# Moving taps of a 31-tap convolution on VectorE from the query and key units into the steps of a top-64 choice

## The chip, the cores and the metric

The kernel runs on one NeuronCore of a Trainium2 chip. A core has a matrix engine (PE, TensorE, with its weight loads as PEld), a vector engine (DVE), a scalar engine (ACT), a general engine (POOL, GpSimd) and a queue engine that issues the DMAs (SP). Each runs its own list of instructions in order and waits for the others by semaphores. The metric is the device time of one execution in microseconds; lower is better.

## What is computed

The reference chains two blocks on a sequence of 256 tokens with 1024 channels. The first block (two layers of modulated attention and feed-forward) is not touched. The second block has two layers; each projects the normed input into many branches. Cut to what matters here:

```python
def second_block(x, positions, ...):
    for l in range(DEPTH):                       # DEPTH = 2
        h = rms_norm(x, g_mix[l])
        proj = h @ w_in[l]
        aq, ak, av, iq, ik, iw, glu_in, cc_in, sb_in, gate_in = jnp.split(proj, offs, axis=-1)
        qa = partial_rope(rms_norm(aq..., g_qa[l]), positions)     # the same for ka
        qi = partial_rope(iq..., positions); ki = partial_rope(rms_norm(ik, g_kidx[l])...)
        y_a = dsa_attention(qa, ka, va, qi, ki, iw) @ w_oa[l]
        glu_a, glu_b = jnp.split(glu_in, 2, axis=-1)
        u = causal_dwconv(glu_a * jax.nn.sigmoid(glu_b), cb_conv_w[l], cb_conv_b[l])   # 31 taps
        y_b = jax.nn.silu(layer_norm(u, cb_ln_g[l], cb_ln_b[l])) @ w_ob[l]
        gb, gc, xc = jnp.split(cc_in, 3, axis=-1)
        y_c = (gb * causal_dwconv(gc * xc, cc_conv_w[l])) @ w_oc[l]                    # 3 taps
        y_d = stick_breaking_attention(...) @ w_od[l]
        ...
```

`dsa_attention` scores all keys by small index heads, keeps the 64 best keys of each query (`lax.top_k`) and does a softmax attention over those. The kernel turns the choice into a mask that is added to the logits.

## The kernel before

Every weight matrix comes from HBM as units of 128 x 2048 float32 values (1 MB, `raw`). ACT rounds a unit to `w_hi` (L1156), DVE subtracts to get the remainder `w_lo` (L1612), and PE multiplies three times for each tile: `h_hi` by `w_hi` (L716), `h_lo` by `w_hi` (L717), `h_hi` by `w_lo` (L718). A unit has 48 such matmuls. There are three slots of `w_hi` and of PSUM banks `ps`, and four of `raw`. ACT and DVE do the split of unit t+2 (`split_ahead`) at the start of their own work on unit t, in program order.

The order of work is a list of stages, the same for each engine, written by `plan_second` for each of the two layers: `glu` (4 units), `cc` (4 and 2), two query units and two key units (`heads`, tiles `aq` and `ak`, which both lie in buffers that the profile calls `spare`), one unit of index queries (`iq`), half a unit of index keys (`ik`), a tiny unit `iw`, two value units (`av`), `select`, four units of plain projections, two of values (`sv`), four of gates, the softmax attention over the chosen keys (`soft`), stick-breaking attention, `layernorm` and so on.

In a `heads` unit ACT copies the product to `kept` (L1324) and squares it, PE makes column sums (L894) and the rotation (L900), ACT makes the reciprocal root `hr`, and DVE multiplies by the cosine (L1875), and one unit later by the sine (L1894, `rope_t`), adds (L1899) and scales by `hr` (L1908). `kept` has two buffers: the copy of unit j waits for L1908 of unit j-2. PE may write a `ps` slot again when L1894 has read it.

The 31-tap convolution works on 512 channels, four tiles of 128. POOL does tiles 2 and 3 in one go from the end of `glu`: for each tap two products (L2354, `cb_product`) and a sum over both (L2360, `cb_sum`). DVE does tiles 0 and 1: for each tap two multiply-add instructions (L2191, L2188 for the first tap) on `cb_sum`, put between its other work by `conv_taps`. How many taps stand at each unit is the tuple of `plan_second`. After its 31 taps POOL goes on with the 3-tap convolution of `cc` (L2354 and L2360 on `cc_sum` and `cc_product`, then L2384, L2386, L2327 with the output `oc_lo`). `cc_product` lies over `cb_in`, the input of the long convolution, so POOL first waits until DVE has done all its taps:

```python
pool.wait_ge(S["conv_first"], s.conv.b["conv_first"] + 2 * CB_TAPS)      # cc on POOL
...
if s.out == "oa":
    dve.wait_ge(S["cc_out"], b["cc_out"])                                # soft on DVE
```

The second wait stands ahead of the first `logits` (L2038) of the softmax attention on DVE.

In `select` DVE sums the scores of two blocks of queries (L2116) and then makes 22 steps on each, called by `each`: eight times MAX8 (L2147), with MATCH_REPLACE8 (L2149) between them, and seven closing steps that make the mask. Odd turns 1 to 15 are the eight MAX8. After each even turn stands the split of one of the ten units that PE multiplies meanwhile (four plain, two value, four gate units, `behind`).

Of the kernel before, what the change touches and what calls it, by code (L numbers as in the profile page):

```python
# [48 lines left out]
CB_TAPS = 31  # L49
# [137 lines left out]
def build(nc, x_t, vecs, consts, positions, cond_rows, ada_first, ada_t, pre_wi, pre_wo, post_wi, post_wo, a_w_qkv, a_w_o, b_w_qkv, b_w_o,  # L187
          w_in, w_oa, w_ob, w_oc, w_od, w_merge, w_gate, w_up, w_down, out):

    def cols_of(w, col0, width, k0=0, kc=KC):  # L190
        def src(j):
            return [(0, w[k0 * P:(k0 + kc) * P, :].rearrange("(k p) m -> p k m", p=P)
                     [:, :, bass.ds(col0 + j * width, width)])]
        return src

    def two_of(wa, ca, wb, cb):
        def src(j):
            return [(0, wa.rearrange("(k p) m -> p k m", p=P)[:, :, bass.ds(ca + j * P, P)]),
                    (P, wb.rearrange("(k p) m -> p k m", p=P)[:, :, bass.ds(cb + j * P, P)])]
        return src  # L200

    unit_done, hi_ready, lo_ready = (nc.alloc_semaphore(n) for n in ("unit_done", "hi_ready", "lo_ready"))
    stages, counts = [], {}
# [30 lines left out]
    def add(run, filler=()):  # L234

        run.t0 = len(units)
        units.extend((run, j) for j in range(run.n))
        run.free = "psum_read_" + run.by
        run.f0 = counts.get(run.free, 0)
        psum_users.extend((run.free, run.f0 + j + 1) for j in range(run.n))  # L240
        counts[run.free] = run.f0 + run.n
        for j in range(run.n):
            program.extend(("chunk", a.first + k) for a, k in share_of(filler, j, run.n))
            program.append(("unit", run.t0 + j))
        return run
# [149 lines left out]
    def plan_second(l, x):  # L395
# [5 lines left out]
        g = Stage("glu", run=add(Run("glu", 4, KC, 2 * P, two_of(w, OFF["glu"], w, OFF["glu"] + 512), "dve", 2)), l=l, h=h)  # L401
        g.takes(glu_sig=4, conv_pad=1, conv_first=2 * CB_TAPS, conv_steps=CB_TAPS, conv_steps_product=CB_TAPS - 1)
        c = Stage("cc", pair=add(Run("cc", 4, KC, 2 * P, two_of(w, OFF["cc"] + 512, w, OFF["cc"] + 1024), "dve", 2)),
                  run=add(Run("cb", 2, KC, 2 * P, cols_of(w, OFF["cc"], 2 * P), "act")), l=l, h=h)
        c.conv = g
        c.takes(cc_gate=4, cc_pad=1, cc_steps=CC_TAPS, cc_steps_product=CC_TAPS - 1, cc_full=4, cc_hi=4, cc_out=4)
        ahead = [len(stages) - 1]
# [10 lines left out]
        Stage("iw", run=add(Run("iw", 1, KC, HEADS2, cols_of(w, OFF["iw"], HEADS2), "act")), h=h)  # L418
        v = value_units(Run("av", 2, KC, 2 * P, cols_of(w, OFF["av"], 2 * P), "act"), 2, "av")
        tap = 0  # L420
        for st, per in zip([c, *stages[ahead[0] + 1:]], (2, 3, 3, 0, 0, 1, 3)):
            runs = (c.pair.n + c.run.n) if st is c else st.run.n
            st.taps = (g, tap, per)
            tap = min(tap + per * runs, CB_TAPS)
        assert tap == CB_TAPS
        sel = Stage("select", waits=[("head_done", k.b["head_done"] + 1), ("psum_read_act", v.run.f0 + 2)])
        sel.takes(iw_turned=1, iw_kept=1, idx_scores=nt * HEADS2, idx_relu=nt * HEADS2, idx_sum=nt * HEADS2, top_steps=nt * 22, sel_mask=nt)

        q = Stage("plain", run=add(Run("sq", 4, KC, 2 * P, cols_of(w, OFF["sb"], 2 * P), "act")), h=h,
# [149 lines left out]
    def con(name):  # L579
        if name in ANGLES:  # L580
            return angles[:, ANGLES.index(name), :]
        o, w = CON[name]
        return con_sb[:, o:o + w]
# [38 lines left out]
    def next_split(u):  # L622

        return Unit(*split_unit(u.t0 + 2)) if u.t0 + 2 < len(units) else None
# [37 lines left out]
    with block:  # L662
# [941 lines left out]
        def _(dve):  # L1604
            def split(u):

                if u is None:
                    return
                n = u.run.kc * u.run.cols
                dve.wait_ge(hi_ready, u.count)  # L1610
                whole, _, _ = raw_of("unit", u.t0)
                nc.vector.tensor_tensor(w_lo[u.low][:, 0:n], whole[:, 0:n], w_hi[u.slot][:, 0:n].bitcast(F32),  # L1612
                                        ALU.subtract).then_inc(lo_ready, 1)

            def split_ahead(u):
                split(next_split(u))
# [490 lines left out]
            def select(s):  # L2107

                b = s.b
                dve.wait_ge(S["iw_kept"], b["iw_kept"] + 1)  # L2110
                for q in range(2):
                    for h in range(HEADS2):
                        i = q * HEADS2 + h
                        dve.wait_ge(S["idx_relu"], b["idx_relu"] + i + 1)
                        before = con("causal")[:, q * SEQ:(q + 1) * SEQ] if h == 0 else idx[:, q, :]
                        nc.vector.scalar_tensor_tensor(idx[:, q, :], rel[:, h, :], iw_sb[:, q, h:h + 1], before, ALU.mult,  # L2116
                                                       ALU.add).then_inc(S["idx_sum"], 1)
                        dve.wait_ge(S["idx_sum"], b["idx_sum"] + i + 1)
                count = [b["top_steps"]]
                last = [0, 0]  # L2120

                def step(q, ins):

                    count[0] += 1
                    last[q] = count[0]
                    ins.then_inc(S["top_steps"], 1)

                def wait_last(q):
                    if last[q]:
                        dve.wait_ge(S["top_steps"], last[q])  # L2130

                behind = [Unit(run, j) for run in s.runs for j in range(run.n)]
                turns = [0]

                def each(body):
                    for q in range(2):
                        wait_last(q)
                        step(q, body(q))
                    turns[0] += 1
                    if turns[0] % 2 == 0 and turns[0] // 2 <= len(behind):  # L2140
                        split_ahead(behind[turns[0] // 2 - 1])

                top = [stats[:, 24 + 8 * q:32 + 8 * q] for q in range(2)]
                cur = [idx[:, q, :] for q in range(2)]
                work = [idx_work[:, q, :] for q in range(2)]
                for r in range(TOPK // 8):
                    each(lambda q: nc.vector.max(top[q], cur[q]))  # L2147
                    if r < TOPK // 8 - 1:
                        each(lambda q: nc.vector.match_replace(work[q], top[q], cur[q], LOWEST))  # L2149
                        cur = work  # L2150
                least = [top[q][:, 7:8] for q in range(2)]
                above = [stats[:, 40 + q:41 + q] for q in range(2)]
                need = [stats[:, 42 + q:43 + q] for q in range(2)]
                gt, eq, cum = ([t[:, q, :] for q in range(2)] for t in (sel_gt, sel_eq, sel_cum))
                each(lambda q: nc.vector.tensor_scalar(gt[q], idx[:, q, :], least[q], None, ALU.is_gt, ALU.add, accum_out=above[q]))
                each(lambda q: nc.vector.tensor_scalar(eq[q], idx[:, q, :], least[q], None, ALU.is_equal))
                each(lambda q: nc.vector.tensor_tensor_scan(cum[q], eq[q], eq[q], 0.0, ALU.add, ALU.max))
                each(lambda q: nc.vector.tensor_scalar(need[q], above[q], -1.0, float(TOPK), ALU.mult, ALU.add))
                each(lambda q: nc.vector.scalar_tensor_tensor(eq[q], cum[q], need[q], eq[q], ALU.is_le, ALU.mult))
                each(lambda q: nc.vector.tensor_tensor(gt[q], gt[q], eq[q], ALU.add))  # L2160
                each(lambda q: nc.vector.tensor_scalar(gt[q], gt[q], -NEG, NEG, ALU.mult, ALU.add))
                for u in behind[turns[0] // 2:]:
                    split_ahead(u)
                for q in range(2):
                    wait_last(q)
                    nc.vector.tensor_tensor(sel_mask[:, q, :], gt[q], con("causal")[:, q * SEQ:(q + 1) * SEQ],
                                            ALU.add).then_inc(S["sel_mask"], 1)
# [10 lines left out]
            def conv_taps(s, i):  # L2178

                    if s.taps is None:  # L2180
                        return
                    conv, first, share = s.taps
                    l, base = conv.l, conv.b["conv_first"]
                    for w in range(min(first + i * share, CB_TAPS), min(first + (i + 1) * share, CB_TAPS)):
                        for c in range(2):
                            x, wcol = cb_in[:, c, w:w + SEQ], vec(f"cb_w{l}", c * CB_TAPS + w)
                            if w == 0:
                                ins = nc.vector.tensor_scalar(cb_sum[:, c, :], x, wcol, vec(f"cb_b{l}", c), ALU.mult, ALU.add)  # L2188
                            else:
                                dve.wait_ge(S["conv_first"], base + 2 * (w - 1) + c + 1)  # L2190
                                ins = nc.vector.scalar_tensor_tensor(cb_sum[:, c, :], x, wcol, cb_sum[:, c, :], ALU.mult, ALU.add)  # L2191
                            ins.then_inc(S["conv_first"], 1)
# [281 lines left out]
```

## Time and profile before

| | us |
|---|---|
| runs | 3072.92, 3076.77, 3082.53 (median 3076.77) |
| the profiled execution | 3075.38 |
| its span from the first to the last instruction | 3073.7 |
| PE busy | 2861.1 (93%) |
| DVE busy | 2010.0 (65%) |
| ACT busy | 1176.9 (38%) |
| POOL busy | 523.2 (17%) |

The profile is of one execution. Busy time is the time in which an engine ran an instruction of its own; the chain of waits follows the work that ended last back from the end, at each step to what released it. A share of the whole span says little about one stage, so most rows below are of one stage: the first layer of the second block, where `glu` ends at 1901 us and the softmax attention starts at 2076 us. The second layer repeats it some 598 us later.

### The profile page before, as it was taken

How to read it: one execution, taken by the hardware profiler on the slowest of the kernel's cores; microseconds unless marked ns; L12 is line 12 of the kernel's file. 1: busy time of each engine (PE TensorE's matmuls, PEld its weight loads, DVE VectorE, ACT ScalarE, POOL GpSimd, SP SyncE). 2: the span in 40 equal slices, each digit the busy share in tenths (PEclk: the TensorE clock that was granted, in tenths of full speed). 3: DMA queues.
4: the chain of work that ended last, by engine and by line, in shares of the span. 5: the costliest groups of instructions: out<-in, count | busy, mean ns of one | idle time of the engine just before them, and what ended most of it. 6: DMA issues, size and time to landing. Idle time of an engine off the chain costs nothing.

```text
span 3073.7 us, 43779 instructions
## 1 busy us (share of the span) xinstructions
PE 2861.1 (93%) x18162; PEld 2552.9 (83%) x18162; DVE 2010.0 (65%) x2974; ACT 1176.9 (38%) x1580; POOL 523.2 (17%) x400
## 2 busy tenths in 40 slices
PE   5999999879999999999789999888989998989999
PEld 3888887759888888888747999887989997989999
DVE  3767754476768676465476656985566779756665
ACT  4212254465222251223445334444444443444433
POOL 0200100010101011010000112991000049700000
PEclk8999999999999999999889999999999998999999
DMA  7556532104556454453202666452556663425555
GB/s 242 181 166 185 164 99 83 56 1 122 167 185 192 130 157 137 142 166 113 70 13 67 183 177 177 121 156 89 161 155 171 172 174 108 144 90 178 157 165 145
DMA packets 593174, 427.39 MB, mean 139 GB/s; under 512 B 16848, under 2 KB 571088, under 8 KB 592720
## 3 DMA queue, kind: packets, MB, share of 16 engines
q1 hardware_dynamic: 592976, 424.59, 46.5%
q8 instruction: 144, 2.36, 0.3%
q14 instruction: 54, 0.44, 0.0%
HBM read 423.50 MB, written 1.05 MB: 138 GB/s over the span
## 4 chain that ended last, share of the span: by engine, by line
PE 66%; POOL 12%; DVE 10%; ACT 7%; DMA 3%; issue 3%; SPq 0%; POOLq 0%; ACTq 0%; DVEq 0%
PE ps L716 19%; PE ps L717 18%; PE ps L718 18%; POOL cb_product L2354 6%; DVE w_lo L1612 5%; ACT w_hi L1156 4%; POOL cb_sum L2360 3%; DVE tap_t L2303 1%; PE pm L1014 1%; PE ps L994 1%; DMA raw<-in_w_in 1%; PE ps L1002 1%; POOL cc_product L2354 1%; PE pm L894 1%; PE ps L917 1%
## 5 line engine op out<-in xcount | busy, mean ns | idle before, releaser
L716 PE MATMUL ps<-h_hi,w_hi 128*128 128x256 f32 (+1 forms) x3744 | 1197.5, 320 | 73.4 <-DVE h_lo L1736 23.5
L717 PE MATMUL ps<-h_lo,w_hi 128*128 128x256 f32 (+1 forms) x3744 | 1187.9, 317 | 0.0
L718 PE MATMUL ps<-h_hi,w_lo 128*128 128x256 f32 (+1 forms) x3744 | 1187.3, 317 | 0.0
L1612 DVE TENSOR_TENSOR w_lo<-raw,w_hi 128x2048 fp32r<-128x2048 f32 (+2 forms) x376 | 809.8, 2154 | 357.2 <-ACT w_hi L1156 354.5
L716 PEld LDWEIGHTS ps<-h_hi,w_hi 128*128 128x128 f32 x3744 | 726.1, 194 | 126.7 <-issue 61.3
L1156 ACT CAST w_hi<-raw 128x2048 fp32r<-128x2048 f32 (+2 forms) x376 | 631.1, 1678 | 489.7 <-PE ps L718 306.6
L717 PEld LDWEIGHTS ps<-h_lo,w_hi 128*128 128x128 f32 x3744 | 726.0, 194 | 43.8 <-issue 0.5
L718 PEld LDWEIGHTS ps<-h_hi,w_lo 128*128 128x128 f32 x3744 | 725.4, 194 | 43.3
L2327 POOL TENSOR_TENSOR act_lo<-sil,act_hi 128x512 fp32r<-128x512 f32 (+1 forms) x132 | 160.1, 1213 | 1955.8 <-DVE act_hi L1850 1390.4
L716 PE MATMUL ps<-act_hi,w_hi 128*128 128x256 f32 (+1 forms) x1122 | 368.9, 329 | 8.2 <-POOL act_lo L2327 8.2
L717 PE MATMUL ps<-act_lo,w_hi 128*128 128x256 f32 (+1 forms) x1122 | 367.7, 328 | 0.0
L718 PE MATMUL ps<-act_hi,w_lo 128*128 128x256 f32 (+1 forms) x1122 | 367.6, 328 | 0.0
L1684 DVE SCALAR_TENSOR_TENSOR dot_t<-chunk_w,cond_all 128x1024 f32<-128x1024 f32 x256 | 311.6, 1264 | 5.7 <-DMA chunk_w<-in_ada_t 5.7
L1304 ACT ACTIVATE sil<-ps 128x512 f32<-128x512 f32 (+1 forms) x88 | 47.8, 544 | 561.7 <-PE ps L718 561.7
L716 PEld LDWEIGHTS ps<-act_hi,w_hi 128*128 128x128 f32 x1122 | 214.6, 191 | 27.8 <-POOL act_lo L2327 9.5
L717 PEld LDWEIGHTS ps<-act_lo,w_hi 128*128 128x128 f32 x1122 | 214.6, 191 | 18.0
L718 PEld LDWEIGHTS ps<-act_hi,w_lo 128*128 128x128 f32 x1122 | 214.6, 191 | 18.0
L2354 POOL TENSOR_SCALAR cb_product<-cb_in,vec_sb 128x256 f32<-128x256 f32 x120 | 172.0, 1443 | 5.9
L1771 DVE SCALAR_TENSOR_TENSOR xs<-ps,mod_sb,xs 128x256 f32<-128x256 f32 x136 | 60.6, 480 | 154.6 <-PE ps L718 154.3
L1848 DVE TENSOR_TENSOR sil<-sil,ps 128x512 f32<-128x512 f32 (+1 forms) x88 | 54.5, 619 | 141.8 <-ACT sil L1304 141.8
L2360 POOL TENSOR_TENSOR cb_sum<-cb_sum,cb_product 128x512 f32<-128x512 f32 x60 | 94.9, 1582 | 5.0
L915 PE MATMUL ps<-w_hi,h_hi 128*128 128x256 f32 x288 | 84.3, 293 | 5.5 <-DVE rope_t L1894 5.5
(276 smaller groups left out, 2997.9 us busy)
## 6 DMA issues: line engine op xcount, KB each, us to landing
chunk_w<-in_ada_t SPq DMA_DIRECT2D x128, 512.0 KB, 3.4
raw<-in_w_in SPq DMA_DIRECT2D x62, 1024.0 KB, 5.4
raw<-in_ffn_pre_wi SPq DMA_DIRECT2D x88, 512.0 KB, 5.3
raw<-in_ffn_post_wi SPq DMA_DIRECT2D x88, 512.0 KB, 5.3
raw<-in_ffn_pre_wo SPq DMA_DIRECT2D x32, 704.0 KB, 4.6
raw<-in_ffn_post_wo SPq DMA_DIRECT2D x32, 704.0 KB, 4.7
raw<-in_w_ffn_gate SPq DMA_DIRECT2D x44, 512.0 KB, 4.0
raw<-in_w_ffn_up SPq DMA_DIRECT2D x44, 512.0 KB, 5.3
```

The lines of the kernel that those rows point to most:

```text
L716: pe.matmul(o, hi, x_hi[:, k, tok], start=k == 0, stop=False)
L717: pe.matmul(o, hi, x_lo[:, k, tok], start=False, stop=False)
L718: return pe.matmul(o, weights(w_lo[u.low], u, k, m * P, P), x_hi[:, k, tok], start=False, stop=k == u.run.kc - 1)
L915: pe.matmul(o, h_hi[:, k, tok], hi, start=k == 0, stop=False)
L1156: nc.scalar.copy(w_hi[u.slot][:, 0:n], whole[:, 0:n]).then_inc(hi_ready, 1)
L1612: nc.vector.tensor_tensor(w_lo[u.low][:, 0:n], whole[:, 0:n], w_hi[u.slot][:, 0:n].bitcast(F32), ALU.subtract).then_inc(lo_ready, 1)
L1684: nc.vector.scalar_tensor_tensor(dot_t[st], chunk_w[n % 2], 1.0, cond_all[:, st, :], ALU.mult, ALU.mult, accum_out=mod_sb[s.layer][:, at_f ...
L1771: last = nc.vector.scalar_tensor_tensor(xs[:, c, tok], o, mod_sb[layer][:, which * KC + c, st:st + 1], xs[:, c, tok], ALU.mult, ALU.add)
L1848: nc.vector.tensor_tensor(sil[:, r, 0:N], sil[:, r, 0:N], ps[u.slot][:, 1, 0:N], ALU.mult).then_inc(S[run.free], 1)
L2327: nc.gpsimd.tensor_tensor(o, whole, hi.bitcast(F32), ALU.subtract).then_inc(S[signal], 1)
L2354: ins = nc.gpsimd.tensor_scalar((product if w else dst)[:, c, :], x, weights_of(c, w), None, ALU.mult)
L2360: nc.gpsimd.tensor_tensor(dst[:, chunks, :], dst[:, chunks, :], product[:, chunks, :], ALU.add).then_inc(S[signal], 1)
```

## The change

Two edits. The taps at each query and key unit go from three to one, and `select` gets a tap of its own after each odd turn as long as taps are left. The sum of both tables is 31: before 6 units of `cc` by 2, 4 units by 3, `iw` 1, two value units by 3; after 6 by 2, 4 by 1, `iw` 1, 2 by 3, and the last 8 in `select`. The assertion on the sum goes.

```diff
@@ plan_second
-        for st, per in zip([c, *stages[ahead[0] + 1:]], (2, 3, 3, 0, 0, 1, 3)):
+        for st, per in zip([c, *stages[ahead[0] + 1:]], (2, 1, 1, 0, 0, 1, 3)):
             runs = (c.pair.n + c.run.n) if st is c else st.run.n
             st.taps = (g, tap, per)
             tap = min(tap + per * runs, CB_TAPS)
-        assert tap == CB_TAPS
         sel = Stage("select", waits=[...])
+        sel.taps = (g, tap, 1)
@@ select on DVE, in each()
                     turns[0] += 1
                     if turns[0] % 2 == 0 and turns[0] // 2 <= len(behind):
                         split_ahead(behind[turns[0] // 2 - 1])
+                    elif turns[0] % 2:
+                        conv_taps(s, turns[0] // 2)
```

Only DVE's list changes its order. The lines behind the edit are two numbers higher: L2191 of before is L2193 of after, L2147 is L2149, L2149 is L2151, L2155 is L2157.

DVE before, a key unit (`spare_102` holds `ak`, `w_lo_53<-raw_49` is the split two units ahead):

```order
 L1612 TENSOR_TENSOR w_lo_53<-raw_49,w_hi_57 128x2048
 L1875 SCALAR_TENSOR_TENSOR spare_102<-kept,vec_sb,con_sb 128x256 x2
-L2191 SCALAR_TENSOR_TENSOR cb_sum<-cb_in,vec_sb,cb_sum 128x256 x6
+L2193 SCALAR_TENSOR_TENSOR cb_sum<-cb_in,vec_sb,cb_sum 128x256 x2
 L1894 TENSOR_TENSOR rope_t<-ps,con_sb 128x256 x2
 L1899 TENSOR_TENSOR spare_102<-spare_102,rope_t 128x2x256
```

Four of the six multiply-adds have left the unit; so it is at each of the four query and key units.

DVE in `select`, the first two MAX8 and the split between them:

```order
-L2147 MAX stats<-idx 128x8 x2
-L2149 MATCH_REPLACE idx_work<-stats,idx 128x256 x2
+L2149 MAX stats<-idx 128x8 x2
+L2193 SCALAR_TENSOR_TENSOR cb_sum<-cb_in,vec_sb,cb_sum 128x256 x2
+L2151 MATCH_REPLACE idx_work<-stats,idx 128x256 x2
 L1612 TENSOR_TENSOR w_lo_56<-raw_52,w_hi_58 128x2048
-L2147 MAX stats<-idx_work 128x8 x2
-L2149 MATCH_REPLACE idx_work<-stats,idx_work 128x256 x2
+L2149 MAX stats<-idx_work 128x8 x2
+L2193 SCALAR_TENSOR_TENSOR cb_sum<-cb_in,vec_sb,cb_sum 128x256 x2
+L2151 MATCH_REPLACE idx_work<-stats,idx_work 128x256 x2
```

Two multiply-adds now stand behind each of the eight pairs of MAX8.

DVE at the last of them:

```order
 L1612 TENSOR_TENSOR w_lo_54<-raw_50,w_hi_58 128x2048
-L2147 MAX stats<-idx_work 128x8 x2
-L2155 TENSOR_SCALAR sel_gt,stats<-idx,stats 128x256 x2
+L2149 MAX stats<-idx_work 128x8 x2
+L2193 SCALAR_TENSOR_TENSOR cb_sum<-cb_in,vec_sb,cb_sum 128x256 x2
+L2157 TENSOR_SCALAR sel_gt,stats<-idx,stats 128x256 x2
 L1612 TENSOR_TENSOR w_lo_55<-raw_51,w_hi_59 128x2048
```

The last tap, for which POOL waits ahead of its short convolution, stood ahead of the index scores (L2116) and now stands behind the eighth pair of MAX8.

## Rows read from the trace of the kernel before

**Rows 1.** The page: busy us by engine, and the chain of waits by line.

```profile
PE 2861.1 (93%) x18162; PEld 2552.9 (83%) x18162; DVE 2010.0 (65%) x2974; ACT 1176.9 (38%) x1580; POOL 523.2 (17%) x400
...
PE ps L716 19%; PE ps L717 18%; PE ps L718 18%; POOL cb_product L2354 6%; DVE w_lo L1612 5%; ACT w_hi L1156 4%; POOL cb_sum L2360 3%; DVE tap_t L2303 1%; PE pm L1014 1%; PE ps L994 1%; DMA raw<-in_w_in 1%; PE ps L1002 1%; POOL cc_product L2354 1%; PE pm L894 1%; PE ps L917 1%
```

**Rows 2.** Chain of waits (start, us, what): POOL's first and last piece.

```profile
1901.45 1.09 POOL cb_sum L2352 x2
...
2075.71 0.75 POOL oc_lo L2327
```

**Rows 3.** DVE's timeline (start, us, instruction, idle before): first `logits`, both layers.

```profile
2076.48 0.43 DVE L2038 SCALAR_TENSOR_TENSOR logits<-ps,sel_mask 128x256 f32<-128x256 f32 x1 [1.91 <-POOL oc_lo L2327]
...
2675.14 0.42 DVE L2038 SCALAR_TENSOR_TENSOR logits<-ps,sel_mask 128x256 f32<-128x256 f32 x1 [2.59 <-POOL oc_lo L2327]
```

**Rows 4.** Stretches: us, busy PE, PEld, DVE, ACT, POOL, granted clock, DMA, GB/s.

```profile
1941.00:1978.00 37.00, 32.39 (x229) 30.59 (x228) 36.80 (x49) 12.05 (x17) 35.40 (x27) 0.95 0.34 90
...
2008.00:2014.00 6.00, 2.13 (x10) 2.13 (x11) 5.75 (x9) 3.33 (x5) 5.64 (x6) 0.58 0.01 1
...
2678.00:2681.00 3.00, 3.00 (x16) 3.00 (x16) 2.33 (x2) 1.39 (x4) 0.00 (x0) 0.50 0.00 0
```

**Rows 5.** ACT's timeline: the index query unit's copy, then the reciprocal root.

```profile
1978.57 0.59 ACT L1324 COPY kept<-ps 128x512 f32<-128x512 f32 x1 [7.52 <-DVE spare L1908]
1979.06 0.69 ACT L1143 ACTIVATE hr<-pm,con_sb 128x512 f32<-128x512 f32 x1
1979.78 0.63 ACT L1145 ACTIVATE hr<-hr 128x512 f32<-128x512 f32 x1
```

**Rows 6.** DVE's timeline in `select`: first, third, fourth split, and the eighth MAX8.

```profile
2016.01 3.11 DVE L1612 TENSOR_TENSOR w_lo<-raw,w_hi 128x2048 fp32r<-128x2048 f32 x1
...
2027.81 2.31 DVE L1612 TENSOR_TENSOR w_lo<-raw,w_hi 128x2048 fp32r<-128x2048 f32 x1 [2.03 <-ACT w_hi L1156]
...
2033.57 2.35 DVE L1612 TENSOR_TENSOR w_lo<-raw,w_hi 128x2048 fp32r<-128x2048 f32 x1 [2.00 <-ACT w_hi L1156]
...
2053.06 0.75 DVE L2147 MAX8 stats<-idx_work 128x8 f32<-128x256 f32 x2
```

**Rows 7.** One tile's instructions: DVE's taps, xcount: min/median/max ns, first and last start.

```profile
L2191 DVE SCALAR_TENSOR_TENSOR cb_sum<-cb_in,vec_sb,cb_sum x120: 471/693/1527, 1907.8 to 2605.8; 128x256 f32<-128x256 f32 x120
```

**Rows 8.** PE's timeline: column sums behind three units (query, key, index query).

```profile
1945.43 0.38 PE L894 MATMUL pm<-sq,con_sb 128*128 128x256 f32 x1
...
1952.90 0.38 PE L894 MATMUL pm<-sq,con_sb 128*128 128x256 f32 x1
...
1974.33 0.59 PE L894 MATMUL pm<-sq,con_sb 128*128 128x256 f32 x2
```

**Rows 9.** DVE's timeline: the first key unit's taps, sine, sum; the last key scaling.

```profile
1961.18 4.91 DVE L2191 SCALAR_TENSOR_TENSOR cb_sum<-cb_in,vec_sb,cb_sum 128x256 f32<-128x256 f32 x6
1966.01 0.74 DVE L1894 TENSOR_TENSOR rope_t<-ps,con_sb 128x256 f32<-128x256 f32 x2
1966.79 0.69 DVE L1899 TENSOR_TENSOR spare<-spare,rope_t 128x512 f32<-128x512 f32 x1
...
1982.61 0.85 DVE L1908 TENSOR_TENSOR spare<-spare,hr 128x512 f32<-128x512 f32 x1
```

**Rows 10.** POOL's timeline: beside DVE's taps, beside a split, beside neither; the last sum.

```profile
1944.61 1.99 POOL L2354 TENSOR_SCALAR cb_product<-cb_in,vec_sb 128x256 f32<-128x256 f32 x2
1946.68 3.10 POOL L2360 TENSOR_TENSOR cb_sum<-cb_sum,cb_product 128x512 f32<-128x512 f32 x1
...
2032.40 1.82 POOL L2354 TENSOR_SCALAR cb_product<-cb_in,vec_sb 128x256 f32<-128x256 f32 x2
...
2039.08 1.29 POOL L2360 TENSOR_TENSOR cb_sum<-cb_sum,cb_product 128x512 f32<-128x512 f32 x1
```

**Rows 11.** DVE's timeline: the first step of `layernorm` in either layer.

```profile
2144.57 0.42 DVE L2263 TENSOR_SCALAR ln_stat<-pm 128x256 f32<-128x256 f32 x1 [2.09 <-PE pm L1118]
...
2744.53 0.42 DVE L2263 TENSOR_SCALAR ln_stat<-pm 128x256 f32<-128x256 f32 x1 [2.09 <-PE pm L1118]
```

## The prediction

> **What bounds the kernel now.** I read the page first. PE is busy 93% of the span, and its dense matmuls are 55% of the chain of waits; yet the long convolution on POOL, an engine that is busy for 17% only, is 9% of it (`cb_product` 6, `cb_sum` 3) [rows 1]. The change touches just the stretch that feeds that part, so I went to the chain of the first layer in order of time. From 1901.45 to 2076.46 every piece is POOL's: the long convolution, then the short one, with no other engine between [rows 2]. Behind it comes DVE's first `logits`, and DVE's timeline says the same: DVE was through with `select` at 2074.57 and stood idle for 1.91 us until POOL's `oc_lo`; in the second layer for 2.59 us [rows 3]. So POOL's list ends last, and DVE's and PE's list runs some 2 us inside it. Whatever makes DVE and PE reach the softmax earlier is worth nothing unless POOL also ends earlier.
>
> In the query and key units DVE is the slow one: busy 36.80 of 37 us, with PE busy 32.39 at a granted clock of 0.95 [rows 4]. ACT's copy of the index query unit waited 7.52 us for DVE's scaling, since `kept` has two buffers [rows 5]. In `select` it is the reverse: the splits start 5.76 us apart, at PE's pace, and DVE is idle 2.0 us before each [rows 6].
>
> **What leaves the query and key units.** Sixteen multiply-adds per layer go (two tiles by two taps by four units), at 0.69 us in the middle [rows 7] and 0.82 at one key unit (six in 4.91 us) [rows 9]: 11 to 13 us of DVE time. DVE then no longer sets the pace, so I follow PE. PE's column sums stood 7.47 us apart where nothing held it (1945.43 to 1952.90) [rows 8]: a unit and its sums. With DVE out of the way the next ones start at 1960.4 and 1967.8, the latter instead of 1974.33. The copy of the index query unit, which stood at 1978.57 because of DVE, follows at about 1968.0; the two `hr` steps (0.69 and 0.63) then end at 1970.3, and L1894, L1899, L1908 (0.74, 0.69, 0.85) at about 1972.7 [rows 5, 9]. Before, that scaling ended at 1983.46. The remainder, 10.76, less some tenths for POOL's sums in between, makes 10.5: DVE and PE are then **10.5 us ahead**; between there and the index scores DVE's list is unchanged and full, so I carry 10.5 us to the start of `select`, with ends of 6.5 (PE's own shift, 1974.33 against 1967.8) and 12.5 (all the tap time).
>
> **What enters select.** Each pair of MAX8 gets two multiply-adds behind it. That is 1.4 to 1.6 us a pair, and up to 2.2 where one of them meets a sum of POOL (the longest took 1.53) [rows 7, 9]. DVE's idle time of 2.0 us before each split covers that; the few tenths that are not covered make a split late. PE wants a unit 5.76 us after the one before, and the split that starts at 2027.81 and ends at 2030.12 is for a unit two further on [rows 6], so nothing of PE waits. Cost on DVE and PE: zero. Without that cover it would be 8 by 1.6, 13 us a layer.
>
> **POOL, the list that counts.** It is not moved, but it shares something with DVE. Two products took 1.82 us beside no split and no tap and 1.99 us beside taps; a sum took 1.29 us and, beside a split, 3.10 us [rows 10]. So a tap costs POOL hardly anything (0.17 us for two products), wherever it stands, and a split costs POOL 1.8 to 1.9 us if it falls while POOL works. Before and after, the same splits and the same taps fall between 1901.45 and POOL's end, for DVE ends `select` before POOL ends either way. They only come earlier. Therefore POOL's total is unchanged, except for one wait.
>
> That wait is the new one: POOL's short convolution waits for DVE's last tap. Before, the last tap was done at 2008.3, ahead of the index scores, 32 us before POOL asked for it at 2040.4 [rows 10]. Now it stands behind the eighth pair of MAX8, which ended at 2053.81 [rows 6]. Shifted by 10.5 us that is 2043.3; with the pair of multiply-adds (1.4 to 2.2) and up to half a microsecond of lateness 2044.7 to 2046.0. POOL asks at: 2040.4 plus the splits that now fall in its long convolution. Before, four splits of `select` did (2016.01 to 2033.57 [rows 6]); 10.5 us earlier and still 5.76 apart there are seven, three by 1.9 is 5.6, so 2046.0. The two meet. I take a wait of 0.5 us in the first layer, and the same in the second: **+1 us**, from 0 to 3.
>
> Here the Trainium skill speaks (SBUF — State Buffer, Who interferes with whom): a DVE instruction with two SBUF inputs and a POOL instruction that reads SBUF share a port pair; whoever starts first keeps it for the whole instruction and the other is blocked. A tap has two SBUF inputs, `cb_in` and `cb_sum`. For the split the trace agrees (1.29 against 3.10 us); for the taps it shows DVE as the one that waits.
>
> **What PE's longer wait costs.** PE will be ready for the softmax some 10.5 us earlier and wait for POOL. After PE's wait ahead of the plain units the granted clock was 0.58 from 2008 to 2014 (the 1.2 GHz level for most of it), and from 2678 to 2681 it was 0.50, right after the softmax's start in the second layer, where in the first layer it was not [rows 4]. From `logits` to `layernorm` the first layer took 68.09 us and the second 69.39 [rows 3, 11]: such a stretch of low clock cost 1.3 us. With 12 to 13 us of idle PE ahead of the softmax I expect one in both layers, perhaps twice as long: +1.3 to +3 in the first, 0 to +1.7 in the second. I take **+3 us**.
>
> **Sum.** 0 for DVE and PE, +1 for POOL's wait, +3 for the clock: a span of 3077.7 instead of 3073.7. The profiled execution took 3075.38, 1.39 below the median of the three runs, so against the median I say 3076.8 + 4 = **3080.8 us**, no difference that can be told. About 0.3%, 9.2 us here, is what a measurement of this kernel can tell from no change.
>
> **Rivals.**
> 1. *POOL waits for the last tap* (slower). It decides by how far DVE is ahead when `select` starts. Every microsecond less than 10.5 puts the last tap a full one later, but POOL's question a third of one earlier, since a split falls out of it every 5.76 us. At 6.5 us ahead the last tap ends at 2048.7 to 2050 and POOL asks at 2040.4 + 2 by 1.9 = 2044.2: a wait of about 5 us a layer. With the clock: 3076.8 + 10 + 3 = **3090 us**. For it: it takes only a lateness of DVE in `select`, where taps behind a POOL sum can take 1.5 us. Against: `kept` and PE set the pace as worked out above, and DVE's idle 2.0 us can catch up. Chance 0.18.
> 2. *Each tap holds POOL back now.* In the key units POOL ran back to back and every tap had to wait for it. If in `select` a tap comes first, POOL waits for the whole of it, 0.47 us at the shortest [rows 7], and sixteen of them cost POOL 7.5 us a layer that it did not pay before: 3076.8 + 15 + 3 = 3095 us. By the Trainium skill's port rule, named above, this is possible. Against it: two products beside taps 1.99 us, not 2.8 [rows 10]. Chance 0.04.
> 3. *The gain comes through* (faster). If the wait that the trace puts on POOL were in truth another one (an inferred releaser), 10.5 us a layer would be won, 3056 us. Or POOL itself gets shorter, because splits fall into its pauses and cost 1.2 instead of 1.9 us (an estimate: a split of 2.3 with the rest of a product over it): for half of the some 18 splits of a layer 6.3 us, so 3076.8 - 12.6 + 3 = 3067 us. Against: POOL has no gap from 1901.45 to 2076.46, and the wait for `cc_out` is written in the code ahead of the first `logits`. Chance 0.07.
> 4. *Nothing moves*, because DVE's time in the query and key units was not what held PE there. Then the last tap would be at 2055, POOL would wait some 14 us a layer, and the time would be 3076.8 + 28 = 3105 us. Chance 0.01, as DVE has no idle time there.
>
> **How the numbers follow.** The forecast, within 0.3%, has a chance of 0.70 and a range of its own from 3074 to 3086: waits of 0 to 3 and clock of 0 to 5, less some 3 us by which splits may fall luckier on POOL. Rivals 1, 2 and 4 lie above 3086 with 0.23, less a little of rival 1 that ends below it and a little of the forecast that ends above. Rival 3 lies below 3067.6 with 0.06. The range is 3072 to 3092: it leaves out rival 3, rival 2 and the upper part of rival 1, under 2 in 10. Faster 0.06, same 0.72, slower 0.22.
>
> **What the profile of the changed kernel would show.** DVE no longer full in the query and key units, and PE's column sums 7.5 us apart. The first MAX8 10.5 us earlier than 2014.56. DVE's idle time before the splits of `select` down from 2.0 to about 0.5 us. POOL's `oc_lo` again the releaser of the first `logits`, at 2076 to 2079, after an idle time of DVE of 11 to 13 us. POOL's first `cc_sum` after the last tap, with a wait of under 1.5 us. A granted clock of 0.5 for 3 to 7 us behind the first `logits` in both layers. I am wrong if POOL's wait for the last tap is over 4 us, if POOL's end moves by more than 4 us, or if something other than POOL releases the first `logits`.

## The result and the profile after

The changed kernel takes 3084.9 us (median of 10 runs, 3078.15 to 3088.55) against 3077.19 us before (10 runs, 3072.92 to 3082.78). The ratio is 1.0021, with a 95% interval of 1.0011 to 1.0031: 3 to 10 us slower, clear of chance, and too little to matter. The forecast was 3080.8 us with a range of 3072 to 3092. The profiled execution of after has a span of 3082.9 us, 9.2 over the one of before.

The page of after, busy time and chain, where [rows 1] stands for before:

```profile
PE 2855.2 (93%) x18162; PEld 2550.0 (83%) x18162; DVE 1994.7 (65%) x2974; ACT 1178.0 (38%) x1580; POOL 529.5 (17%) x400
...
PE ps L716 19%; PE ps L717 19%; PE ps L718 19%; POOL cb_product L2356 7%; DVE w_lo L1612 4%; ACT w_hi L1156 3%; POOL cb_sum L2362 3%; PE pm L1014 1%; PE ps L994 1%; DMA raw<-in_w_in 1%; DVE tap_t L2305 1%; PE ps L1002 1%; PE pm L894 1%; PE ps L917 1%; PE ps L916 1%
```

DVE is busy 15 us less though it does the same work. Its 120 multiply-adds of the long convolution make 11.4 us of that (86.7 us before, 75.3 now): a tap that does not have to wait for POOL is short. POOL is busy 6 us more though its list is untouched, and its products have gone from 6 to 7% of the chain.

Busy time by stretch (the stretch and its length in us, then busy PE, PEld, DVE, ACT, POOL, granted clock, DMA, GB/s). The first line is of the query and key units, the other two are ahead of and behind the first `logits`:

```profile
1938.00:1975.00 37.00, 36.56 (x274) 34.32 (x273) 34.39 (x46) 18.60 (x25) 35.46 (x27) 1.00 0.47 131
2063.00:2076.00 13.00, 0.00 (x0) 0.00 (x0) 0.00 (x0) 0.00 (x0) 12.23 (x16) 0.61 0.00 0
2077.00:2083.00 6.00, 4.76 (x19) 4.04 (x20) 4.66 (x10) 3.15 (x6) 0.00 (x0) 0.51 0.01 3
```

In the query and key units PE is now busy 36.56 of 37 us, where it was 32.39 in [rows 4], at full clock. The won time then lies in one heap: from 2063 to 2076 nobody works but POOL. POOL's timeline, the last piece ahead of the first `logits`, and DVE's, the first `logits` of both layers (compare [rows 2, 3]):

```profile
2076.04 0.72 POOL L2329 TENSOR_TENSOR oc_lo<-cc_sum,oc_hi 128x256 fp32r<-128x256 f32 x1
...
2076.80 0.42 DVE L2038 SCALAR_TENSOR_TENSOR logits<-ps,sel_mask 128x256 f32<-128x256 f32 x1 [18.30 <-POOL oc_lo L2329]
...
2683.70 0.42 DVE L2038 SCALAR_TENSOR_TENSOR logits<-ps,sel_mask 128x256 f32<-128x256 f32 x1 [18.28 <-POOL oc_lo L2329]
```

DVE's idle time ahead of `logits` went from 1.91 and 2.59 us to 18.30 and 18.28. And this is how a step of `select` and POOL's taps beside it look now, to be held against [rows 6, 10]:

```profile
2028.56 0.86 DVE L2193 SCALAR_TENSOR_TENSOR cb_sum<-cb_in,vec_sb,cb_sum 128x256 f32<-128x256 f32 x2
...
2030.67 2.98 DVE L1612 TENSOR_TENSOR w_lo<-raw,w_hi 128x2048 fp32r<-128x2048 f32 x1 [0.47 <-ACT w_hi L1156]
2033.57 0.74 DVE L2149 MAX8 stats<-idx_work 128x8 f32<-128x256 f32 x2
2034.24 0.86 DVE L2193 SCALAR_TENSOR_TENSOR cb_sum<-cb_in,vec_sb,cb_sum 128x256 f32<-128x256 f32 x2
...
2028.74 1.38 POOL L2356 TENSOR_SCALAR cb_product<-cb_in,vec_sb 128x256 f32<-128x256 f32 x1
2030.20 1.30 POOL L2362 TENSOR_TENSOR cb_sum<-cb_sum,cb_product 128x512 f32<-128x512 f32 x1
2031.60 4.21 POOL L2356 TENSOR_SCALAR cb_product<-cb_in,vec_sb 128x256 f32<-128x256 f32 x2
2035.89 1.29 POOL L2362 TENSOR_TENSOR cb_sum<-cb_sum,cb_product 128x512 f32<-128x512 f32 x1
```

The pair of taps takes DVE 0.86 us, not 1.4 to 1.6. POOL pays: the single product at 2028.74, which meets the pair that starts at 2028.56, takes 1.38 us, where two undisturbed ones took 1.82, 0.92 each [rows 10]. The two products at 2031.60 meet the split at 2030.67 and the pair at 2034.24.

To compare layers and executions I measure from POOL's first `cb_sum` of the layer (`start`). POOL's long convolution, its whole list to the last `oc_lo`, the end of DVE's last tap and the end of the mask, all in us from there, worked out from the timelines:

| kernel, layer | long convolution | last `oc_lo` | last tap | mask | `layernorm` |
|---|---|---|---|---|---|
| before, 1 | 138.9 | 175.0 | 107.0 | 173.1 | 243.1 |
| before, 2 | 141.1 | 175.6 | 107.0 | 173.0 | 245.0 |
| after, 1 | 150.2 | 178.4 | 142.4 | 160.2 | 247.8 |
| after, 2 | 150.4 | 178.8 | 142.3 | 160.6 | 248.7 |

POOL's list is 3.4 and 3.2 us longer. From the first `logits` to `layernorm` it is 69.35 and 69.84 us instead of the 68.09 and 69.39 of [rows 3, 11], 1.7 together. That is 8.3 us; the rest of the 9.2 is drift of other stages, which took 3.1 us less ahead of the first layer and 3.7 us more between the two.

### The profile page after: what moved, and what is told of

Same layout as the page of the kernel before. It is cut to its first block, busy times and chain, and to the rows that moved or that the text cites. A ratio compares the mean times of both kernels' runs of the same rounds, so it can differ in the third digit from the quotient of the medians.

```text
span 3082.9 us, 43779 instructions
## 1 busy us (share of the span) xinstructions
PE 2855.2 (93%) x18162; PEld 2550.0 (83%) x18162; DVE 1994.7 (65%) x2974; ACT 1178.0 (38%) x1580; POOL 529.5 (17%) x400
## 3 DMA queue, kind: packets, MB, share of 16 engines
HBM read 423.50 MB, written 1.05 MB: 138 GB/s over the span
## 4 chain that ended last, share of the span: by engine, by line
PE 68%; POOL 12%; DVE 9%; ACT 6%; DMA 3%; issue 3%; SPq 0%; POOLq 0%; ACTq 0%; DVEq 0%
PE ps L716 19%; PE ps L717 19%; PE ps L718 19%; POOL cb_product L2356 7%; DVE w_lo L1612 4%; ACT w_hi L1156 3%; POOL cb_sum L2362 3%; PE pm L1014 1%; PE ps L994 1%; DMA raw<-in_w_in 1%; DVE tap_t L2305 1%; PE ps L1002 1%; PE pm L894 1%; PE ps L917 1%; PE ps L916 1%
## 5 line engine op out<-in xcount | busy, mean ns | idle before, releaser
L2356 POOL TENSOR_SCALAR cb_product<-cb_in,vec_sb 128x256 f32<-128x256 f32 x120 | 203.4, 1705 | 5.9
L2362 POOL TENSOR_TENSOR cb_sum<-cb_sum,cb_product 128x512 f32<-128x512 f32 x60 | 84.1, 1401 | 5.0
```

Source lines behind the costliest of these rows:

```text
L2356: ins = nc.gpsimd.tensor_scalar((product if w else dst)[:, c, :], x, weights_of(c, w), None, ALU.mult)
L2362: nc.gpsimd.tensor_tensor(dst[:, chunks, :], dst[:, chunks, :], product[:, chunks, :], ALU.add).then_inc(S[signal], 1)
```

## Experiments

**1 and 2: is it the taps in `select`, or the splits that come earlier?** Theory P: the pair of taps holds POOL up, since it has two inputs in SBUF. Theory S: the earlier splits fall worse on POOL. The first run leaves the eight taps out, so DVE is ahead but `select` is as before; this kernel and that of run 2 lack a part of the convolution and serve for timing alone.

```diff
-        sel.taps = (g, tap, 1)
...
-                    elif turns[0] % 2:
-                        conv_taps(s, turns[0] // 2)
```

> The changed kernel with its eight taps per layer in select left out (tiles 0 and 1 of the long convolution lack taps 23 to 30, and the waits for the last tap ask for 23 taps). DVE gets as far ahead as in the changed kernel, but nothing stands between the steps of the choice. POOL's list from its first cb_sum to its last oc_lo took 175.0 and 175.6 us before and 178.4 and 178.8 after. Theory P (a tap between the steps holds POOL up): about 175 in both layers, total 6 to 7 us under the changed kernel, 3077 to 3079, so the gain in the query and key units still gives nothing. Theory S (the splits, which now come 11 us earlier, fall worse on POOL): still 178 to 179, total near 3085. In either case DVE waits 16 us or more for oc_lo ahead of the first logits.

Measured: 3077.01 us, ratio to before 0.9994 (0.9984 to 1.0005). POOL's list took 172.9 and 173.6 us, 5.5 and 5.3 less than in the changed kernel and 2.1 and 2.0 less than before. One part of the expectation missed: DVE waited 12.1 us ahead of `logits`, not 16 or more, since POOL's list was the shorter one and the mask ended no earlier than in the changed kernel (160.8 and 161.5 us from the start).

The second run puts two MAX8 of a finished tile where each pair of taps was, one input in SBUF instead of two.

```diff
+                    elif turns[0] % 2 and turns[0] < 16:
+                        for c in range(2):
+                            nc.vector.max(stats[:, 48 + 8 * c:56 + 8 * c], cb_sum[:, c, :])
```

> As e1_no_select_taps (the same taps left out), with two MAX8 of a finished tile of cb_sum in the place of each pair of taps: about the same DVE time (0.8 us a pair) but one input in SBUF instead of two. Theory P, the port pair: POOL's list about 175 us again, as in e1, products beside the inserted pair at 0.92 us, total 3077 to 3079. Theory T (the inserted time makes the splits late, and that is what POOL feels): 178 us, products as long as in the changed kernel, total near 3085.

Measured: 3076.54 us, ratio 0.9991 (0.9982 to 1.0000); POOL's list 174.0 and 173.5 us. The timelines of DVE and POOL in this run, to be read against those of after above:

```profile
2021.41 0.74 DVE L2143 MAX8 stats<-cb_sum 128x8 f32<-128x256 f32 x2
...
2033.77 0.73 DVE L2143 MAX8 stats<-cb_sum 128x8 f32<-128x256 f32 x2
2034.48 0.40 DVE L2151 MATCH_REPLACE8 idx_work<-stats,idx_work 128x256 f32<-128x256 f32 x1
...
2021.62 1.29 POOL L2362 TENSOR_TENSOR cb_sum<-cb_sum,cb_product 128x512 f32<-128x512 f32 x1
...
2031.12 3.75 POOL L2356 TENSOR_SCALAR cb_product<-cb_in,vec_sb 128x256 f32<-128x256 f32 x2
```

The same DVE time (0.74 us against 0.86) in the same place costs POOL nothing. The sum at 2021.62 meets the extra pair at 2021.41 and takes the 1.29 us of an undisturbed one. The two products at 2031.12 meet a split and the extra pair at 2033.77 and take 3.75 us; in the kernel before two products that met a split alone took as long:

```profile
2017.07 3.75 POOL L2354 TENSOR_SCALAR cb_product<-cb_in,vec_sb 128x256 f32<-128x256 f32 x2
```

In the changed kernel, with a pair of taps there, they take 4.21. So it is not DVE's lateness and not the splits. Theories S and T fall. MAX8 differs from a tap in one more thing, as it writes 8 values for each partition and not 256. MATCH_REPLACE8 reads one tile from SBUF and writes all 256: the one at 2034.48 falls on the last of these products, and they take no more than 3.75 us.

What a pair costs POOL can be read in two ways. By the rows it is 0.46 us (4.21 against 3.75, or 1.38 against 0.92), 3.7 us for eight. By the whole list, the changed kernel against run 1, it is 5.4 us for eight, 0.68 us each; what makes up the other 1.7 us no run separates. The list of run 1 is 2.05 us shorter than before. That holds what the eight pairs had cost in the query and key units, 0.26 us each at most if nothing else is in it, but it also holds the earlier splits, and it is no more than the 2.0 us by which layers of the unchanged kernel differ (runs 9 and 10 below).

**3: the pairs alone.** The kernel before with sixteen multiply-adds more per layer in `select`; its taps stay where they were.

```diff
+                    elif turns[0] % 2 and turns[0] < 16:
+                        for c in range(2):
+                            nc.vector.scalar_tensor_tensor(sel_cum[:, c, :], cb_sum[:, c, :], 1.0,
+                                                           cb_sum[:, 1 - c, :], ALU.mult, ALU.add)
```

> The kernel before with 16 more multiply-adds per layer in select, two behind each odd turn up to the fifteenth, on finished tiles of cb_sum into a scratch tile (all 31 taps stay where they were). DVE is not ahead here. Theory P: only the pairs that fall on POOL's work count, and all eight do (2014 to 2055 us, POOL ends at 2076): 8 by 0.46 us is 3.7 us of POOL a layer, 178 to 179 us for its list, total 5 to 8 us over before, 3082 to 3085. Theory S: POOL's list stays at 175 us, total as before within 2 us.

Measured: 3086.81 us, ratio 1.0026 (1.0015 to 1.0036), 8 to 10 us over before, where 5 to 8 was expected. POOL's list took 178.9 and 178.8 us, 3.6 over the mean of 175.2 in four layers of before: 0.45 us a pair. Here DVE is not ahead at all, and the slowdown of the changed kernel is there in full. POOL's timeline and DVE's:

```profile
2027.38 4.09 POOL L2357 TENSOR_SCALAR cb_product<-cb_in,vec_sb 128x256 f32<-128x256 f32 x2
...
2030.03 0.73 DVE L2144 SCALAR_TENSOR_TENSOR sel_cum<-cb_sum 128x256 f32<-128x256 f32 x2
```

Two products that meet a split and a pair take 4.09 us where they took 3.75 with MAX8 in that place. Theory P holds.

**4: what the wait for the last tap would cost.** My first rival said that POOL might wait there. In the result it does not: the last tap ends 142.4 us from the start, and POOL asks at 150.2. This run moves the last tap of each layer behind the mask.

```diff
-                    elif turns[0] % 2:
+                    elif turns[0] % 2 and turns[0] < 15:
...
                     nc.vector.tensor_tensor(sel_mask[:, q, :], gt[q], ...)
+                conv_taps(s, 7)
```

> The changed kernel with only the last tap of each layer moved from behind the eighth MAX8 to behind the mask, which moves its end from 2041 to about 2059 us. It prices the wait of my first rival. If POOL's short convolution waits for the last tap: its first cc_sum at 2059 to 2060 instead of 2048.7, with no splits left to disturb it 23 to 24 us from there to the last oc_lo instead of 28, so POOL's list is 5 to 7 us longer in each layer, total 10 to 13 us over the changed kernel, 3095 to 3098. If that wait is not what starts the short convolution, the time stays near 3085.

Measured: 3098.03 us, ratio 1.0061 (1.0046 to 1.0076). POOL's timeline and DVE's:

```profile
2058.37 3.63 POOL L2357 TENSOR_SCALAR cc_sum<-cc_in,vec_sb 128x256 f32<-128x256 f32 x4 [10.71 <-DVE cb_sum L2194]
...
2082.26 0.42 DVE L2038 SCALAR_TENSOR_TENSOR logits<-ps,sel_mask 128x256 f32<-128x256 f32 x1 [24.09 <-POOL oc_lo L2330]
```

POOL stands 10.71 us, and its list is 5.7 and 6.0 us longer (184.1 and 184.8), as expected; 13.1 us in the medians. The mechanism of the rival is real; its deadline was 8 us away in the changed kernel.

**5 and 6: is the gain real, and held by POOL's end?** Theory G says that the softmax waits for POOL by one wait alone. What it guards is memory: `oa` lies over `cb_in` and `cc_product`. The first `oa` is written 12.9 us after the first `logits`, so the wait can stand there.

```diff
                 def chunk_out(chunk):
+                    if s.out == "oa" and chunk == 0:
+                        dve.wait_ge(S["cc_out"], b["cc_out"])
...
-                if s.out == "oa":
-                    dve.wait_ge(S["cc_out"], b["cc_out"])
```

On the kernel before:

> The kernel before with DVE's wait for cc_out moved from ahead of the first logits to ahead of the first write of oa_hi, the first that lands where POOL still works. Theory G (POOL's end holds the softmax, and by this wait alone): DVE gains the 1.9 and 2.6 us that it stood idle, total 3 to 5 us less, 3072 to 3074. If something else holds it, no difference.

Measured: 3068.88 us, ratio 0.9973 (0.9962 to 0.9983), some 7 us less, where 3 to 5 was expected (a miss, taken up in runs 9 and 10). `layernorm` starts 241.0 and 241.1 us from the start.

On the changed kernel:

> The changed kernel with the same move. Theory G: the 11 us won in the query and key units come through, up to the second wait: logits at 2059 to 2061 instead of 2076.8, the first oa_hi some 13 us on would be 2073, but waits for oc_lo at 2078 to 2080 (POOL now shares its last part with the softmax). Against 2089.8 in the changed kernel 10 to 12 us a layer, total 3061 to 3065. Rival: PE and DVE are held by something else on the way, and less than 5 us a layer comes through (3075 or more).

Measured: 3055.78 us, ratio to before 0.9935 (0.9920 to 0.9950), 29 us less than the changed kernel without the move and 5 us below the expected 3061 to 3065. DVE's timeline:

```profile
2057.22 0.42 DVE L2038 SCALAR_TENSOR_TENSOR logits<-ps,sel_mask 128x256 f32<-128x256 f32 x1 [0.17 <-PE ps L994]
...
2079.55 0.42 DVE L1647 CAST oa_hi<-pm 128x256 fp32r<-128x256 f32 x1 [6.51 <-POOL oc_lo L2328]
```

Its waits (total us, count, mean us), both layers:

```profile
DVE oa_hi L1647 <- POOL oc_lo L2328: 13.0, 2, 6.5
```

The 18.3 us in front of `logits` are gone, and 6.5 us remain in front of `oa_hi`. I had expected POOL's end at 2078 to 2080 and it came at 2079.5, 4.3 us later in its list (182.7) than in the changed kernel, with the softmax now running beside it. `layernorm` starts 12.6 us earlier in each layer (235.2, 236.1 us from the start), where 10 to 12 was expected.

**7 and 8: the wait gone altogether.** `oa` gets a place that is free as soon as the long convolution is done.

```diff
-    branch = {n: tuple(over(f"{n}_{half}", 16 + 8 * i + 4 * k, ...
+    branch = {n: tuple(over(f"{n}_{half}", kb, (4, SEQ), F32R) for half, kb in zip(("hi", "lo"), at_kb))
+              for n, at_kb in (("oa", (20, 24)), ("ob", (16, 28)), ("oc", (32, 36)), ("od", (40, 44)))}
...
                     if s.out == "oa" and chunk == 0:
-                        dve.wait_ge(S["cc_out"], b["cc_out"])
+                        dve.wait_ge(S["conv_steps"], b["conv_steps"])
```

> As e6_after_late_wait, with oa moved to a place that POOL has left after the long convolution (oa at 20 to 28 KB, ob_hi at 16 KB), and the wait asking for the long convolution only. Theory G: no wait of the softmax for POOL at all, the first oa_hi at 2073 to 2075, 15 to 16 us a layer less than in the changed kernel, total 3053 to 3057. If e6 already got all of it, the same time as e6.

Measured: 3048.81 us, ratio to before 0.9916 (0.9900 to 0.9933), 4 us below the expected 3053 to 3057. DVE's timeline:

```profile
2056.77 0.42 DVE L2038 SCALAR_TENSOR_TENSOR logits<-ps,sel_mask 128x256 f32<-128x256 f32 x1 [0.18 <-PE ps L994]
...
2072.48 0.42 DVE L1647 CAST oa_hi<-pm 128x256 fp32r<-128x256 f32 x1
```

No wait is left in front of either. This version beats both kernels, by 27 us the one before (medians of the same series, 3048.81 against 3075.94). The same moves without the change:

> The kernel before with the same two moves as e7_after_oa_moved. Theory G: as e5, 3 to 5 us less than before, 3072 to 3074, since before DVE reached the softmax only 1.9 and 2.6 us ahead of POOL. The difference between e8 and e7 is then what taking the taps out of the query and key units is worth once POOL's end holds nobody: about 11 us a layer less what taps in select cost there, 18 to 22 us. If it is under 10 us, the gain in the query and key units was not real.

Measured: 3068.28 us, ratio to before 0.9977 (0.9967 to 0.9987), again 4 us below the expected 3072 to 3074. Between runs 7 and 8 stands only the change of this study, and it is worth 19.5 us there, in the expected 18 to 22.

**9 and 10: how much of it is chance.** In runs 5 and 8 the long convolution took 137.5 us in both layers, in the first profile of before 138.9 and 141.1, and there was a surplus in run 5 to explain. Both kernels once more, unchanged:

> The kernel before, unchanged, profiled once more. In the two profiles with only the wait moved (e5, e8) the long convolution on POOL took 137.5 us in both layers, in the profile of before 138.9 and 141.1, though nothing differs ahead of it but a tenth of a microsecond between POOL and DVE. If this is chance of an execution (theory C), the long convolution here may again be anything from 137 to 141.5 us and differ between the layers, and the surplus of e5 over the 3 to 5 us expected is the same kind of chance. If it is fixed by the kernel, 138.9 and 141.1 again within 0.3.

Measured: 3079.3 us; the long convolution 139.1 and 137.5 us, POOL's list 176.1 and 174.1. Not fixed by the kernel, then, and theory C holds for before: 174.1 to 176.1 in four layers.

> The changed kernel, unchanged, profiled once more. In the four profiles with these taps in select (after, e4, e6, e7) the long convolution took 149.4 to 150.6 us. Theory C says that here POOL and DVE run in step (a tap of POOL takes 5.7 us, a split of DVE comes every 5.76), so it should again be 149.4 to 150.6 in both layers, and the last oc_lo 178 to 179 us after the first cb_sum. Otherwise it spreads as widely as before.

Measured: 3084.42 us; the long convolution 151.2 and 145.2 us, POOL's list 179.6 and 176.5. Here the expectation missed: the second layer fell out of step, and its long convolution was 5 us shorter than in the other layers. There the first three pairs of taps in `select` meet a sum of POOL, for instance

```profile
2615.32 1.47 DVE L2193 SCALAR_TENSOR_TENSOR cb_sum<-cb_in,vec_sb,cb_sum 128x256 f32<-128x256 f32 x2
...
2615.99 1.88 POOL L2356 TENSOR_SCALAR cb_product<-cb_in,vec_sb 128x256 f32<-128x256 f32 x2
```

Here DVE is the one that waits, 1.47 us for a pair instead of 0.86, and the two products behind it take 1.88 us, 0.06 over undisturbed ones. The four layers of after stand at 176.5 to 179.6, mean 178.3, those of before at a mean of 175.2; they do not overlap, and 3.1 us a layer is the difference. For the surplus of run 5: `layernorm` came 3.0 us a layer earlier than the mean of 244.0 of before's four layers, 6 us in all, of which its two waits, 1.9 and 2.6 us, are 4.5. Most of the other 1 to 2 us can be seen: in runs 5 and 8 the first MAX8 stands at 111.5 to 111.7 us in all four layers, as in the second layer of run 9, and at 113.1 to 113.3 in the other three layers of before; the mask of run 5 ends 0.9 us a layer sooner than their mean. Run 9 shows that the unchanged kernel can do this by chance. Whether four layers of four are chance too is not shown.

## Why the prediction was right, point by point

- **POOL's list ends last and holds the softmax.** Right, and shown by runs 5 to 8: without that wait the same change is worth 19.5 us. `oc_lo` is again the releaser, after 18.3 us, where I had written 11 to 13. The figure was short by two things. DVE reached the end of the mask 13 us earlier (160.2 against 173.1), not 10.5: 11.1 at the first MAX8, and the last steps of `select`, from the start of the last split to the end of the mask, took 4.6 us instead of 6.2. And POOL's list was 3.4 us longer; 1.9, 13.0 and 3.4 make the 18.3.
- **Query and key units at PE's pace, 10.5 us ahead.** Right. PE's column sums stand 7.47 us apart, as worked out from [rows 8]:

```profile
1949.80 1.02 PE L894 MATMUL pm<-sq,con_sb 128*128 128x256 f32 x4
1957.27 1.02 PE L894 MATMUL pm<-sq,con_sb 128*128 128x256 f32 x4
1964.74 1.02 PE L894 MATMUL pm<-sq,con_sb 128*128 128x256 f32 x4
```

  The first MAX8 comes 102.04 us from the start instead of 113.11, 11.1 us earlier.
- **Taps in `select` covered by DVE's idle time.** Right: the idle time before a split, 1.1 to 2.0 us before (none ahead of the first split), is 0.15 to 0.54 us in the first layer and 0.67 to 1.05 in the second, and in the profile PE never waited for a split in `select`.
- **POOL pays no more for a tap there than elsewhere.** Wrong; this is the term of the sum that failed. I read 0.17 us for two products beside taps from [rows 10], from a place where DVE and POOL both run without a pause, and took it for the price of a tap wherever it stands. In `select` a pair costs 0.46 us by the rows, 0.45 in run 3, and 0.68 by the whole list in the changed kernel. The term "POOL's total unchanged" should have been +3.3 us a layer, 6.6 in all. It was my second rival, which I gave 0.04, at half its size: not both taps of a pair but one of them is waited for, 0.46 us on the product that meets it (1.38 against 0.92).
- By the Trainium skill (SBUF — State Buffer, Who interferes with whom), an instruction with two SBUF inputs shares the port pair with POOL's reads, and issue order, not the shape of the operation, decides who blocks. I had let the row overrule it. Runs 2 and 3 agree on the two inputs: 3.75 us for two products that meet a split and MAX8, 4.09 with a pair of multiply-adds instead. Run 10 agrees on the order: the same pair of taps is stretched to 1.47 us where it meets a running sum, and takes 0.86 us where POOL pays. My rows showed one order, and the change made mostly the other.
- **POOL's wait for the last tap, +1 us.** It was 0. The last tap came at 142.4 where I had 143.3 to 144.6 from the start, and POOL asked at 150.2, not at 144.6: I had counted three more splits in its long convolution, 5.6 us, and it grew by 11.3. Eight splits of `select` fell in it (2002.63 to 2042.43) where four had; an estimate from the rows, four by 1.9 us and eight pairs by 0.46, gives the 11.3. What the long convolution lost the short one got back: 28.0 us instead of 35.9.
- **The clock, +3 us.** From `logits` to `layernorm` it was 1.7, which I put down to the clock; no run separates it. The granted clock was 0.51 from 2077 to 2083, as expected, but in the second layer before such a stretch had been there already.
- **The sum.** 0 + 1 + 3 = 4 forecast; 0 + 6.6 + 1.7 = 8.3 found in the profiles, and 3 to 10 us in the runs. The mechanism that decides the outcome was right. Its smaller terms were wrong in opposite directions, so that the time came out as near the forecast as it did is in part luck.

## What to carry to other kernels

Before moving work off an engine that looks full, follow the chain to the next point where all lists meet, and see whose list ends there: here 11 us a layer were won on two engines and lost in the wait for a third that nobody had touched, and moving one wait that guarded a buffer took 29 us off the changed kernel. When one engine's list is the last, every instruction that shares a port with it is priced by that list, and a price read from one place in a trace is the price of that order of issue only. Look first at what a wait guards: moving the work alone cost 8 us, moving the buffer and its wait alone gave 8, and both together gave 27.

## What the runs showed of the hardware

- Who waits, DVE or POOL, depends on what the tap meets. In [rows 10] DVE's taps are stretched (up to 1.53 us [rows 7]) and POOL's products go by at 0.97 to 1.03 us. In `select` of the changed kernel a pair that starts in the last tenth of a product takes DVE 0.86 us and costs the next product 0.46 us; in run 10 a pair that meets a running sum takes DVE 1.47 us and costs the two products behind it 0.06. MAX8 stands ahead of the taps in both, so it is not what decides.
- The two engines can fall in step. In the changed kernel a tap of POOL with one split and one pair of taps takes 5.69 us (4.21 for the products, 1.29 for the sum, two pauses of 0.1), and the splits come every 5.76 us; so nearly every tap of POOL in `select` meets a split and a pair. Partly out of step, as in the second layer of run 10, the same work took 145.2 instead of 150.4 us.
- The same kernel does not always take the same time there. In the kernel before, unchanged, POOL's long convolution took 137.5, 139.1, 138.9 or 141.1 us.
